# Two more modulation pieces on VectorE among the input units, and half of the first gate summed by GpSimd and ScalarE

## The reference

```python
x = layer_norm(x, emb_ln_g, emb_ln_b)
cs = silu(c)
sh1, sc1, gt1, sh2, sc2, gt2 = split(cs @ w_ada + b_ada, 6)    # each 1024 long
p = (x * (1.0 + sc1) + sh1) @ w_in                             # 1024 -> 2848
y_a = gmlp_spatial_gating(p[:, :512], p[:, 512:1024], ...)
y_b = rwkv7_time_mix(p[:, 1024:], ...)                         # 8 heads of 64, a recurrence over the rows
x = layer_norm(ALPHA * x + gt1 * (concat(y_a, y_b) @ w_out), ln1_g, ln1_b)
gu = (x * (1.0 + sc2) + sh2) @ w_ffn_in
x = layer_norm(ALPHA * x + gt2 * ((silu(gu[:, :2816]) * gu[:, 2816:]) @ w_ffn_out), ln2_g, ln2_b)
```

## Time and profile before

| what | value |
|---|---|
| median of 3 runs | 1401.75 us |
| the profiled execution | 1400.58 us |
| its span, first to last instruction | 1398.5 us |
| mean granted clock of TensorE | 0.991 |
| busy: TensorE, VectorE, ScalarE, GpSimd | 95%, 53%, 42%, 34% |
| moved by DMA | 147.92 MB, 106 GB/s on average |

### The profile page before, as it was taken

The page is one execution under the profiler, slowest core; times in us unless marked ns, Lnnn a source line. Parts: engine busy times, 40 slices in busy tenths (PEclk is TensorE's granted clock), DMA queues, the critical chain, the costliest instruction groups (busy, mean ns, idle before and its releaser), DMA issues.

```text
span 1398.5 us, 22604 instructions
## 1 busy us (share of the span) xinstructions
PE 1327.2 (95%) x9338; PEld 1104.1 (79%) x9338; DVE 745.6 (53%) x1227; ACT 587.6 (42%) x895; POOL 475.4 (34%) x139
## 2 busy tenths in 40 slices
PE   3999988979899999999999999999999999999998
PEld 2778877767788888888888787777798888888886
DVE  7677798554765444354236547797256444542002
ACT  7544574363442232221226445655364344333212
POOL 4433242633223344444432310000213334443444
PEclk8999999999999999999999999999999999999999
DMA  9554101322213333224213511101312322223211
GB/s 376 223 208 169 61 3 45 135 98 82 100 61 136 136 120 120 91 94 146 91 64 120 218 61 36 57 31 61 105 61 91 114 97 90 91 95 131 91 61 60
DMA packets 25900, 147.92 MB, mean 106 GB/s; under 512 B 2848, under 2 KB 4000, under 8 KB 11208
## 3 DMA queue, kind: packets, MB, share of 16 engines
q1 hardware_dynamic: 22272, 134.21, 27.0%
q10 hardware_dynamic: 3528, 12.28, 2.3%
HBM read 144.36 MB, written 4.74 MB: 107 GB/s over the span
## 4 chain that ended last, share of the span: by engine, by line
PE 79%; DVE 12%; ACT 4%; issue 2%; POOL 2%; DMA 1%; SPq 0%; DVEq 0%; ACTq 0%
PE bank L2247 23%; PE bank L2249 23%; PE bank L2248 23%; PE bank L2509 4%; PE bank L1214 1%; ACT weight_hi L1429 1%; PE bank L1207 1%; DVE xres L1790 1%; PE bank L1198 1%; POOL weight_lo L1367 1%; POOL xres L1410 1%; DVE bank L1783 1%; DVE acc L1011 1%; DVE pv L1787 1%; DVE act_lo L1787 1%
## 5 line engine op out<-in xcount | busy, mean ns | idle before, releaser
L1367 POOL TENSOR_TENSOR weight_lo<-raw,weight_hi 128x2048 fp32r<-128x2048 f32 (+2 forms) x84 | 389.2, 4634 | 802.6 <-ACT weight_hi L1429 802.6
L2247 PE MATMUL bank<-act_hi,weight_hi 128*128 128x512 f32 (+1 forms) x1136 | 434.2, 382 | 15.8 <-DVE act_lo L1787 10.5
L2249 PE MATMUL bank<-act_hi,weight_lo 128*128 128x512 f32 (+1 forms) x1136 | 423.7, 373 | 0.0
L2248 PE MATMUL bank<-act_lo,weight_hi 128*128 128x512 f32 (+1 forms) x1136 | 423.5, 373 | 0.0
L1429 ACT ACTIVATE weight_hi<-raw 128x2048 fp32r<-128x2048 f32 (+1 forms) x98 | 185.3, 1891 | 404.7 <-PE bank L2249 394.5
L2247 PEld LDWEIGHTS bank<-act_hi,weight_hi 128*128 128x128 f32 x1136 | 214.4, 189 | 62.6 <-issue 18.5
L2249 PEld LDWEIGHTS bank<-act_hi,weight_lo 128*128 128x128 f32 x1136 | 214.1, 189 | 38.5
L2248 PEld LDWEIGHTS bank<-act_lo,weight_hi 128*128 128x128 f32 x1136 | 214.5, 189 | 35.0 <-issue 0.5
L2247 PE MATMUL bank<-weight_hi,hid_hi 128*128 128x512 f32 x352 | 136.9, 389 | 0.0
L2248 PE MATMUL bank<-weight_lo,hid_hi 128*128 128x512 f32 x352 | 136.9, 389 | 0.0
L2249 PE MATMUL bank<-weight_hi,hid_lo 128*128 128x512 f32 x352 | 136.9, 389 | 0.0
(11 more groups left out here) (402 smaller groups left out, 1897.6 us busy)
## 6 DMA issues: line engine op xcount, KB each, us to landing
raw<-in_weights SPq DMA_DIRECT2D x112, 1024.0 KB, 4.8
first_piece<-in_first_ada SPq DMA_DIRECT2D x15, 512.0 KB, 15.5
w<-in_w ACTq DMA_DIRECT2D x2, 2048.0 KB, 11.5
bias_rows<-bias_rows_once ACTq DMA_DIRECT2D x1, 2560.0 KB
xres<-in_x SPq DMA_DIRECT2D x4, 512.0 KB, 6.8
strip<-bias_rows ACTq DMA_DIRECT2D x1, 2048.0 KB, 8.0
out<-xres SPq DMA_DIRECT2D x3, 512.0 KB, 2.6
row_a<-in_ln_g ACTq DMA_DIRECT2D x2, 512.0 KB, 4.2
```

The lines of the kernel that those rows point to most:

```text
L1367: pool.tensor_tensor(wlo[i % SPLIT][:, :size], raw[n % RAW][:, :size], whi[i % SPLIT][:, :size], ALU.subtract).then_inc(lo_ready, 1)
L2247: pe.matmul(o, l[0], r[0], start=first, stop=False)
L2248: pe.matmul(o, l[0], r[1], start=False, stop=False)
L2249: return pe.matmul(o, l[1], r[0], start=False, stop=last)
```

## The change

Two more units of the second modulation (ada1_4 and ada1_5) are loaded among the input units, behind pv0 and pv1, and summed by VectorE, beside v1 and pv0, so six in all instead of four. The units left over, ada1_6 and ada1_7, are now loaded between ada2_1 and ada2_2. GpSimd and ScalarE still have four units in the second pair group: these two, and then ada2_2 and ada2_3 (half of the first gate). VectorE's `first_gate` shrinks from four units to two, both behind stage ta of the second pair group; its job behind m2 and z4 of the first pair group and the one behind n of the second are gone. Since ScalarE's accumulator doesn't start from the bias, a job `gate_bias` on VectorE adds it to the four late columns, behind stage m2 of the second pair group, and `mod_rows` waits for that.

```diff
--- before.py
+++ after.py
@@ -93,10 +93,10 @@
 
 
 
-ADA_BEHIND = {"r0": 1, "r1": 1, "v0": 1, "v1": 1}
-ADA_BESIDE = {"k1": 1, "r0": 1, "r1": 1, "v0": 1}
+ADA_BEHIND = {"r0": 1, "r1": 1, "v0": 1, "v1": 1, "pv0": 1, "pv1": 1}
+ADA_BESIDE = {"k1": 1, "r0": 1, "r1": 1, "v0": 1, "v1": 1, "pv0": 1}
 EARLY_ADA = sum(ADA_BEHIND.values())
-LATE_ADA = [f"ada1_{k}" for k in range(EARLY_ADA, 8)]
+LATE_ADA = [f"ada1_{k}" for k in range(EARLY_ADA, 8)] + ["ada2_2", "ada2_3"]
 GATE_AT, GATE_ROWS_AT = (4, 7, 10, 13), 16
 
 
@@ -119,7 +119,7 @@
         n = ADA_BEHIND.get(unit[0], 0)
         units += second[:n]
         second = second[n:]
-    units += gates[0] + second
+    units += gates[0][:2] + second + gates[0][2:]
     units += [(f"out1_{n}", "w_out", 2 * n * P, 2, ((0, DM),)) for n in range(4)]
     for m in range(FT):
         units.append((f"up1_{m}", "w_ffn_in", 0, KC, ((m * P, P), (FFN + m * P, P))))
@@ -328,11 +328,11 @@
         ("r3", 0): [("prep", 3, 6), ("prep", 3, 7), ("sgu", 1)],
         ("r3", 1): [("prep", 3, 4), ("prep", 3, 8), ("sgu", 2)],
         ("m", 0): [("prep", 3, 9), ("sgu", 3)], ("m", 1): [("prep", 3, 10), ("prep", 3, 11)],
-        ("m2", 0): [("prep", 3, 12), ("prep", 0, 13)], ("m2", 1): [("prep", 1, 13), ("ada", 0, 0)], ("z4", 1): [("ada", 0, 1)]},
-    1: {("ta", 1): [("ada", 1, 0), ("ada", 1, 1), ("ada", 2, 0), ("ada", 2, 1)], ("n", 1): [("ada", 3, 0), ("ada", 3, 1)],
-        ("mv", 0): [("prep", 2, 13), ("ada_rows", 0)], ("q2", 0): [("ada_rows", 1)], ("q2", 1): [("ada_sums", 0), ("ada_rows", 2)],
+        ("m2", 0): [("prep", 3, 12), ("prep", 0, 13)], ("m2", 1): [("prep", 1, 13)]},
+    1: {("ta", 1): [("ada", 0, 0), ("ada", 0, 1), ("ada", 1, 0), ("ada", 1, 1)], ("n", 1): [("ada_rows", 0)],
+        ("mv", 0): [("prep", 2, 13)], ("q2", 0): [("ada_rows", 1)], ("q2", 1): [("ada_sums", 0), ("ada_rows", 2)],
         ("q4", 0): [("prep", 3, 13)], ("q4", 1): [("ada_sums", 1), ("ada_rows", 3)], ("tb", 0): [("ada_sums", 2)],
-        ("tb", 1): [("ada_sums", 3)]}}
+        ("tb", 1): [("ada_sums", 3)], ("m2", 1): [("gate_bias",)]}}
 AT_END = {("q4", 1): [("norm", 0, 0), ("norm", 1, 0)], ("r2", 0): [("norm", 0, 1), ("norm", 0, 2)],
           ("r2", 1): [("norm", 1, 1), ("norm", 1, 2)], ("tb", 1): [("norm", 0, 3), ("norm", 0, 4)],
           ("r3", 0): [("norm", 1, 3), ("norm", 1, 4), ("norm", 0, 5)], ("m", 0): [("norm", 0, 6), ("norm", 1, 5)],
@@ -1386,8 +1386,6 @@
                 norm_side(o, args[0])
             elif kind == "ada_rows":
                 n = UNIT_AT[LATE_ADA[args[0]]]
-                if args[0] == 0:
-                    pool.wait_ge(S["gate_sums"], KC // 2)
                 raw_ready(pool, n)
                 for j in range(2):
                     w = raw[n % RAW][:, DM * j:DM * j + DM]
@@ -1651,7 +1649,8 @@
             elif kind == "ada_sums":
                 i = args[0]
                 k = EARLY_ADA + i
-                for j, total in enumerate((affine[:, 3, k:k + 1], modc[:, KC + k:KC + k + 1])):
+                totals = (affine[:, 3, k:k + 1], modc[:, KC + k:KC + k + 1]) if k < KC else [gate_cols[:, 0, 2 * i + j:2 * i + j + 1] for j in range(2)]
+                for j, total in enumerate(totals):
                     w = raw[UNIT_AT[LATE_ADA[i]] % RAW][:, DM * j:DM * j + DM]
                     act.wait_ge(S["ada_rows"], 2 * i + j + 1)
                     a.done(act.activation(w, w, ACT.Copy, accum_out=total), S["ada_summed"])
@@ -2107,6 +2106,10 @@
                 norm_dve(*args)
             elif kind == "ada":
                 first_gate(*args)
+            elif kind == "gate_bias":
+                dve.wait_ge(S["ada_summed"], 2 * len(LATE_ADA))
+                late, b = gate_cols[:, 0, KC // 2:KC], COLS["b_gt1"]
+                tt(late, late, pc[:, b + KC // 2:b + KC], ALU.add, sem=S["gate_sums"])
             elif kind == "mixer" and args[0] == 0:
                 dve.wait_ge(S["y_hi"], 1)
                 tt(act_lo[:, 0:2, :], uT[:, 0:2, :], act_hi[:, 0:2, :].bitcast(F32), ALU.subtract, sem=S["y_lo_first"])
@@ -2686,7 +2689,7 @@
         def mod_rows(j):
 
             claim(pe, ("mod_rows", j))
-            pe.wait_ge(S["gate_sums"], 2 * j + 2)
+            pe.wait_ge(S["gate_sums"], 2 + j)
             across(("mod_rows", j), lambda i: gate_cols[:, 0, 4 * j + i:4 * j + i + 1], 4)
 
         begun = []
@@ -2724,7 +2727,7 @@
         for m in range(2, FT):
             dense_feature(f"up1_{m}", 2)
             if m == GATE_ROWS_AT:
-                pe.wait_ge(S["gate_sums"], KC)
+                pe.wait_ge(S["gate_sums"], 3 + KC // 2)
                 for j in range(2):
                     claim(pe, ("gate_rows", j))
                     across(("gate_rows", j), lambda i: gate_cols[:, 1, 4 * j + i:4 * j + i + 1], 4)
```

## The result

| | kernel before | changed kernel |
|---|---|---|
| median (20 runs each, the same chip) | 1401.53 us | 1404.21 us |
| lowest to highest | 1397.96 to 1405.16 us | 1401.75 to 1410.49 us |
| profiled execution, its span | 1400.58, 1398.5 us | 1402.99, 1401.0 us |

The ratio is 1.0030, with a 95% interval of 1.0019 to 1.0040: slower by 4.2 us (2.7 to 5.6); the two medians lie 2.7 us apart, at the lower end of that. Forecast was 1405.2 us, slower by 3.5. Every median and ratio in this document is of executions at the usual pace: two of the twelve in "The load behind g2", of 1668.31 and 2671.26 us, are left out.

The account below looks back on a forecast made before the run. TensorE was taken as the bound among the input units, and the first pair group as latency-bound. The terms, 8.2 - 3.0 - 1.7 = +3.5 us, gave 1405.2 us against the median of 1401.75; range 1401 to 1410.

Parts of the forecast that it names:

- The stall: Among the input units, at pu0: TensorE, ready at 150.37 us, starts at 156.36 us, costing 6.0 us.
- The clock behind it: Behind two gaps at pu0: granted clock falls for one or perhaps two stretches, costing 2.2 us (1.7 to 2.8).
- part 1: Two more pieces among the input units: late weights for pu0 and the lower clock cost +8.2 us in sum.
- The sixth piece and pu1: Among the input units: piece beside pv0 precedes a later wait anyway, pu1's split ends before TensorE needs it: 0.
- The gap at g2: First pair group, 234.71 to 238.69 us: without the transfer TensorE's gap shrinks from 3.67 to 0.66 us, -3.0 us.
- the slow stretch: First pair group, 239.4 to 242.9 us: the stretch at granted clock 0.51 goes, -1.7 us.
- the twin: Same stage in the second pair group, without a transfer: TensorE stops for 0.66 us, taken as what would remain.
- Part 3: Second pair group: moved pieces, row sums and new addition cost 0; slow stretch at 256.5 us 0, bounds -1.7 and +1.7.
- A: At 235 us the gap doesn't close, or moves: +6.5 to +8.2 us, 1408.3 to 1410 us; chance 17%.
- B: Kinder clock: one slow stretch in the input units, none at 256.5 us: +1.3 us, 1403 us; chance 15%.
- C: At 150.37 us pu0's load isn't late on TensorE, decided by the fifth piece's end (138.9 us): -4.7 us, 1397; 10%.
- part 2: End of the first pair group: ada2_0's halves and a 1 MB transfer leave, worth -3.0 and -1.7 us.

Follow-up runs that it names:

- The load behind g2: Kernel before, with ada2_3's load held until VectorE has drained stage g2 of the first pair group: 1396.99 us (0.9982), again 1395.94 us (0.9969).
- the last experiment: Changed kernel with the fifth piece ahead of preparation step 12 and the first gate wholly on VectorE: 1396.92 us, ratio 0.9980 to the kernel before.
- part 1 alone: Kernel before with six early pieces; ada2_0 keeps its place, first gate wholly on VectorE, two late units on GpSimd and ScalarE: 1406.15 us, ratio 1.0037.
- the first copy: Changed kernel plus an unread 1 MB DRAM-to-DRAM copy, which left at 248.59 us with ada1_7's load: 1406.49 us, ratio 1.0047 to the kernel before.

## Why the prediction came out

**The stall, 6.0 us forecast, 6.1 measured.** Each link was as worked out: the collision went (0.69 us), the piece ended at 142.91 us (144.92 forecast, less 1.99 of lag: 142.93), conversion 5.04 us behind it (4.78), 1.91, 4.51, TensorE 0.06 us later. The second gap was 1.84 us and not 3.1, since the product in the middle took 2.04 us at the low clock instead of 1.02 and came a little later; that moved nothing, as pu0's low part sets the end. The spread of the stall is larger than one profile can show: 5.9, 6.0, 6.0, 6.1, 7.6 and 7.7 us in the six executions that have it, by how soon the conversion followed. To forecast 6.0 for this one took the right links and a hand-over that happened to be of the usual length. The late load alone in the kernel before gives the same cost, and an earlier piece takes it away: this cause is shown, not argued.

**The clock behind it, 2.2 us forecast, 2.8 measured** (8.88 less 6.1; 1.9 to 3.0 in the six executions). The slow stretch was one of 10.2 us (6.8 us in two of the six), not one or two of 3.4. This is the only term of part 1 that was too small: I priced the clock by a single gap of 2 us, and behind two gaps close together it stayed low for longer.

**The sixth piece and pu1, 0.** From 160 to 234 us the lag moves by 0.3 us. What lies behind the slow stretch moves as a whole.

**The gap at g2, -3.0 forecast, -2.5 measured, and the slow stretch, -1.7 and -1.5.** The cause was right: putting a transfer back brings the gap back, and holding the load back in the kernel before takes it away. The size was taken from the twin (0.66 us), but what is left at this place without a transfer is 1.20 us, and 0.8 to 1.5 us over the nine profiles whose loads leave it alone. The packet starts 1.4 to 1.5 us before TensorE stops there, and 1.7 us before in the twin; that is part of the difference to 0.66, the rest is open. The Trainium skill (Runtime: NRT & Kernel Launch, Instruction fetch mechanics) says that the cost of an instruction block is "mostly hidden". The runs don't bear that out here: with a transfer in flight the gap is 3.1 to 3.7 us, and even alone it is about 1.2.

**Part 3, 0 forecast, -0.6 us measured between 260 and 306 us,** and the four halves at "ta" are covered, with 0.88 us to spare. That this was close, and what lies behind it, is shown by the kernel with six halves there.

**The rest is slow stretches that the forecast held at 0.** The three entries of the first table for which no step of the change can be named come to -1.99 - 1.58 + 1.5 = -2.1 us in the profiled pair; with them taken out, its +2.55 us is +4.6. The forecast's steps sum to +3.5, and the runs say +4.2 (2.7 to 5.6). The misses are +0.7 in part 1, +0.5 and +0.2 at g2 and -0.6 in part 3, so they cancel in part. Whether the stretch at 313 us belongs to the change, which would add to its cost, isn't settled. Two of the named signs came out otherwise: the gap at g2 is 1.20 us and not 0.7, and behind 350 us the shift is 2.6 us in the profile and not 3 to 4.

**Rivals.** A (the gap moves): a wait of 1.34 us with no releaser does stand at 252 us, in the burst of the next loads, but the lag is flat there, so it costs nothing; it takes another 1 MB to make it pay. B (a kinder clock) came true at 256.5 us and untrue at pu0 and at 313 us. C was wrong about this change and right about the place: its point of decision held within 0.1 us for hand-overs of the usual length, and with the piece ahead of step 12 the change is the faster kernel. That order alone is worth 5.1 us (seven operations of 0.69 us and their starts); in the first of the two profiles the piece came 7.5 us earlier, as a copy ahead of it took 0.17 us and not 4.19.

## What to carry to other kernels

With a ring of buffers, ask of each added user when it ends, and follow from there: free buffer, transfer, conversion, split, matmul. The work itself was free here (VectorE had room), and the order of two jobs on it decided between +4 and -3 us. In the stage of many small matmuls a transfer of 1 MB cost TensorE 3 to 4 us, though nobody waited for it: its instruction packet came behind the burst. So try to hold a load that isn't urgent back until behind such a stage. And if a part seems to bring nothing in the total, look at the lag along the run before dropping it: 2.8 us were gained at one place and lost at another in the last experiment, and in part 1 alone 2.8 us of gain hid the 4 us that part 2 is worth.

## What was not expected of the hardware

- A copy that no one waits for stopped TensorE for 3.12 us, and the instruction packet came only as the burst ended. A gap of 0.8 to 1.5 us stays without any transfer. In all thirteen profiles TensorE goes on 2.2 to 2.9 us behind the start of the packet, so where a gap at such a stage has the releaser "issue", look for the packet ahead of it. The 1.34 us wait at 252 us is the same (packet at 250.87, on at 253.37 us); the gap of 1.99 us at 65 us isn't, as no packet came in the 17 us ahead of it. Nor does a packet always wait for the end of the data: those at 250.87 us (changed kernel) and 253.97 us (with the first copy) came in the middle of a burst of several megabytes. How the queues share isn't shown.
- From the end of the fifth piece, which frees a raw buffer, to the conversion of the next 1 MB took 4.8 to 5.0 us in six executions and 6.5 and 6.6 us in two. This alone moved the stall by 1.5 us. What makes the difference isn't known.
- Whether the granted clock falls behind one and the same gap differs between executions: behind the same gap of 1.99 us at 65 us it was low for 3.4 us in the kernel before, and not at all in the changed one, both with the same instructions up to there. Each such stretch is worth 1.5 to 2 us, as much as some of the terms above. What decides it was not tried.
